# Norm entries of a fused model: three of eight tiles to GpSimd, branch gain at read-out, double-width weighing on VectorE

## What is computed

```python
def rmsnorm(x, g):
    y = x * rsqrt(mean(x * x, axis=-1) + EPS)
    return y * g

h = h + rmsnorm(mix, g[1])
ff = conv_ffn(rmsnorm(h, g[2]), ffn_w_up[l], ffn_conv[l], ffn_w_down[l])
h = h + rmsnorm(ff, g[3])
```

## Time and profile before

| | |
|---|---|
| median of three runs | 1592.94 us (1592.41 to 1594.91) |
| profiled execution, its own time | 1595.38 us |
| span of its profile | 1593.6 us |
| TensorE busy | 1469.6 us, 92% |
| VectorE busy | 1041.1 us, 65% |
| ScalarE busy | 779.9 us, 49% |
| GpSimd busy | 281.6 us, 18% |
| mean granted clock of TensorE | 0.967 |

### The profile page before, as it was taken

How to read it: one execution, slowest core, us unless ns; L and a number is a source line. 1 busy time by engine, 2 the same in 40 slices (tenths; PEclk the granted TensorE clock), 3 DMA queues, 4 the chain that set the end, 5 groups by cost and what they waited for, 6 DMA issues and landing times. The chain is left out here.

```text
span 1593.6 us, 29023 instructions
## 1 busy us (share of the span) xinstructions
PE 1469.6 (92%) x11301; PEld 1404.5 (88%) x11301; DVE 1041.1 (65%) x1727; ACT 779.9 (49%) x1272; POOL 281.6 (18%) x384
## 2 busy tenths in 40 slices
PE   5999879999788898999998899989999989999997
PEld 4999769999686667999997789989999987899997
DVE  5664678877765447788757755357787665677643
ACT  5655644454454444555545555564443555534341
POOL 0000101220053330121100153102332100132110
PEclk8999999999998899999998999999999998999999
DMA  6432535659431224465771311236765733275451
GB/s 275 176 126 106 192 122 193 233 188 335 177 139 74 80 104 162 166 234 211 255 252 58 132 54 54 68 121 222 277 248 208 242 106 137 99 291 185 145 181 44
DMA packets 41141, 265.80 MB, mean 167 GB/s; under 512 B 4561, under 2 KB 5713, under 8 KB 15441
## 3 DMA queue, kind: packets, MB, share of 16 engines
q1 hardware_dynamic: 41040, 264.44, 46.0%
HBM read 263.38 MB, written 1.05 MB: 166 GB/s over the span
## 5 line engine op out<-in xcount | busy, mean ns | idle before, releaser
L224 DVE TENSOR_TENSOR w_lo<-raw,w_hi 128x2048 fp32r<-128x2048 f32 (+2 forms) x207 | 425.4, 2059 | 238.4 <-ACT w_hi L220 234.7
L220 ACT ACTIVATE w_hi<-raw 128x2048 fp32r<-128x2048 f32 (+3 forms) x224 | 385.8, 1727 | 38.1 <-PE bank L398 34.0
L396 PE MATMUL bank<-z_hi,w_hi 128*128 128x258 f32 x752 | 215.4, 286 | 5.1 <-DVEq L931 4.2
L397 PE MATMUL bank<-z_lo,w_hi 128*128 128x258 f32 x752 | 213.0, 283 | 0.0
L398 PE MATMUL bank<-z_hi,w_lo 128*128 128x258 f32 x752 | 212.3, 282 | 0.0
L396 PE MATMUL bank<-x_hi_up,w_hi 128*128 128x272 f32 (+1 forms) x704 | 203.5, 289 | 8.2 <-DVE x_lo_up L688 8.1
L398 PE MATMUL bank<-x_hi_up,w_lo 128*128 128x272 f32 (+1 forms) x704 | 201.7, 287 | 0.0
L397 PE MATMUL bank<-x_lo_up,w_hi 128*128 128x272 f32 (+1 forms) x704 | 201.4, 286 | 0.0
L396 PEld LDWEIGHTS bank<-z_hi,w_hi 128*128 128x128 f32 x752 | 142.1, 189 | 6.7 <-DVE w_lo L224 3.0
L397 PEld LDWEIGHTS bank<-z_lo,w_hi 128*128 128x128 f32 x752 | 143.2, 190 | 0.1
L398 PEld LDWEIGHTS bank<-z_hi,w_lo 128*128 128x128 f32 x752 | 142.4, 189 | 0.0
(11 more groups left out here) (450 smaller groups left out, 3832.1 us busy)
## 6 DMA issues: line engine op xcount, KB each, us to landing
raw<-w_up SPq DMA_DIRECT2D x44, 1024.0 KB, 4.8
raw<-w_gu SPq DMA_DIRECT2D x44, 1024.0 KB, 4.8
work<-w_ada SPq DMA_DIRECT2D x27, 1024.0 KB, 4.9
raw<-w_down SPq DMA_DIRECT2D x32, 704.0 KB, 4.3
raw<-w_dn SPq DMA_DIRECT2D x32, 704.0 KB, 4.1
raw<-w_a_in SPq DMA_DIRECT2D x16, 1024.0 KB, 5.5
mod_w_down<-w_ada SPq DMA_DIRECT2D x12, 1024.0 KB, 6.2
raw<-w_gdn_qkv SPq DMA_DIRECT2D x12, 1024.0 KB, 4.8
```

Of the source, the lines that this page charges most:

```text
L220: act.activation(w_hi[:, s, 0:blocks * P], raw[:, s, 0:blocks * P], ACT.Copy).then_inc(hi_split.sem, 1)
L224: dve.tensor_tensor(w_lo[:, s, 0:blocks * P], raw[:, s, 0:blocks * P], w_hi[:, s, 0:blocks * P].bitcast(F32), ALU.subtract).then_inc(lo_sp ...
L396: pe.matmul(o, w_hi[:, s, b], x_hi[:, xk, cols[0]:cols[1]], start=begin, stop=False)
L397: pe.matmul(o, w_hi[:, s, b], x_lo[:, xk, cols[0]:cols[1]], start=False, stop=False)
```

## The change

- `branch_out` squares all tiles of an item first and then copies them; the copy carries the branch norm's gain as its scale, so what lies in `work` is already weighed with the gain. A semaphore of its own (`branch_taken`) counts the copies.
- In a `NormEntry`, tiles 5, 6 and 7 are GpSimd's. It multiplies them by rstd and adds them to h (residual part), multiplies the gained tile by rstd, and subtracts to x_lo (operand part). The gain of these tiles is applied by ScalarE in three more copies ahead of it. With a shift, ScalarE also writes the shifted tile back.
- VectorE keeps tiles 0 to 4. In the residual part it weighs and adds tiles 0 and 1, 2 and 3 in one instruction each, and tile 4 alone, with tensor_tensor instead of scalar_tensor_tensor.
- ScalarE squares in the order 5, 0, 1, 6, 2, 3, 4, 7 and rounds in the order 0, 5, 1, 6, 2, 3, 7, 4. TensorE's first tile takes k in the order 0, 1, 5, 2, 6, 3, 4, 7.
- In Fox and Gdn GpSimd's entry work comes ahead of its mask and of its small memsets; in Hgrn it comes behind its memsets.
- Waits for all splits now name both engines' semaphores. The unused variants of `NormEntry` are gone.

```diff
+                            for at, k in enumerate(entry.k_order if opening else range(k_tiles)):
                                 b = slice((t * k_tiles + k) * P, (t * k_tiles + k + 1) * P)
                                 xk = k0 + k
-                                begin = xk == 0
-                                end = xk == (FF_TILES if halves else k_tiles) - 1
-                                if entry and isinstance(r, int) and r == first and t == 0:
-                                    pe.wait_ge(entry.split.sem, entry.split.at(k + 1))
+                                begin = k0 + at == 0
+                                end = k0 + at == (FF_TILES if halves else k_tiles) - 1
+                                if opening:
+                                    entry.part_split(pe, k)
                                 if x_ready and isinstance(r, int) and r <= first + 1:
...
-        branch_squared, branch_summed = sig("branch_squared"), sig("branch_summed")
+        branch_squared, branch_summed, branch_taken = sig("branch_squared"), sig("branch_summed"), sig("branch_taken")
+        BRANCH_GAIN = {"a_out": 1, "down0": 3, "b_out": 5, "down1": 7}
 
         def branch_out(name, tiles, cols, squares, halves):
+            gain_at = BRANCH_GAIN[name] * KD
...
                 for t in range(tiles):
+                    slot = s // 2 if halves else j % 2 * 2 + t
+                    act.activation(squares[:, slot, 0:width], where(t)[:, 0:width], ACT.Square).then_inc(branch_squared.sem, 1)
+                for t in range(tiles):
                     at = (j - 1) // 2 if halves else j * tiles + t
                     d = work[:, at, cols[0]:cols[1]] if isinstance(at, int) else work[:, bass.ds(at, 1), cols[0]:cols[1]]
-                    act.activation(d, where(t)[:, 0:width], ACT.Copy)
-                    slot = s // 2 if halves else j % 2 * 2 + t
-                    last = act.activation(squares[:, slot, 0:width], where(t)[:, 0:width], ACT.Square)
-                    last.then_inc(branch_squared.sem, 1)
-                act.wait_ge(branch_squared.sem, branch_squared.at((j + 1) // 2 if halves else (j + 1) * tiles))
+                    act.activation(d, where(t)[:, 0:width], ACT.Copy,
+                                   scale=par("gains", at + gain_at)).then_inc(branch_taken.sem, 1)
+                act.wait_ge(branch_taken.sem, branch_taken.at((j + 1) // 2 if halves else (j + 1) * tiles))
                 act.sem_inc(item_out.sem, 2 if halves else 1)
...
+                normed = residual
+                mine, theirs = n - 3, (n - 3, n - 2, n - 1)
+                square_order = [5, 0, 1, 6, 2, 3, 4, 7] if residual else list(range(n))
+                high_order, self.k_order = [0, 5, 1, 6, 2, 3, 7, 4], [0, 1, 5, 2, 6, 3, 4, 7]
...
+                def part_split(eng, k):
+                    if k < mine:
+                        eng.wait_ge(x_split.sem, x_split.at(k + 1))
+                    else:
+                        eng.wait_ge(p_x_split.sem, p_x_split.at(k - mine + 1))
+
+                def all_split(eng):
+                    eng.wait_ge(x_split.sem, x_split.at(mine))
+                    eng.wait_ge(p_x_split.sem, p_x_split.at(3))
...
+                    for k in square_order:
+                        if normed and k < mine:
+                            act.wait_ge(h_added.sem, h_added.at(k + 1))
+                        elif normed:
+                            act.wait_ge(p_h_added.sem, p_h_added.at(k - mine + 1))
+                        act.activation(work[:, k, c0:c1], src(k), ACT.Square).then_inc(squared.sem, 1)
+                    if act_first:
+                        act_first(act)
+                    act.wait_ge(summed.sem, summed.at(1))
+                    act.activation(std[:, c0:c1], bank[6][:, 0:c1 - c0], ACT.Sqrt, scale=1.0 / count,
+                                   bias=eps_col[:, 0:1]).then_inc(std_made.sem, 1)
+                    for k in theirs:
+                        act.activation(work[:, k, c0:c1], src(k), ACT.Copy, scale=gain(k)).then_inc(x_gained.sem, 1)
+                    for k in high_order:
+                        if k < mine:
+                            act.wait_ge(x_made.sem, x_made.at(k + 1))
+                        else:
+                            act.wait_ge(p_x_made.sem, p_x_made.at(k - mine + 1))
+                        if shift:
+                            ins = act.activation(x_hi[:, k, x_cols], work[:, k, c0:c1], ACT.Identity, bias=shift(k))
+                            if k >= mine:
+                                ins = act.activation(work[:, k, c0:c1], work[:, k, c0:c1], ACT.Identity, bias=shift(k))
+                        else:
+                            ins = act.activation(x_hi[:, k, x_cols], work[:, k, c0:c1], ACT.Copy)
+                        ins.then_inc(x_high.sem, 1)
                     if act_then:
                         act_then(act)
+
+                def low_part(eng, k):
+                    eng.wait_ge(x_high.sem, x_high.at(high_order.index(k) + 1))
+                    hi = x_hi[:, k, x_cols].bitcast(F32)
+                    if shift and k < mine:
+                        ins = eng.scalar_tensor_tensor(x_lo[:, k, x_cols], work[:, k, c0:c1], shift(k), hi, ALU.add,
+                                                       ALU.subtract)
+                    else:
+                        ins = eng.tensor_tensor(x_lo[:, k, x_cols], work[:, k, c0:c1], hi, ALU.subtract)
+                    ins.then_inc((x_split if k < mine else p_x_split).sem, 1)
...
+                    def weigh(k, m):
+                        dve.tensor_tensor(work[:, k:k + m, c0:c1], work[:, k:k + m, c0:c1],
+                                          rstd[:, c0:c1].unsqueeze(1).broadcast_to([P, m, c1 - c0]),
+                                          ALU.mult).then_inc(weighed.sem, m)
+
+                    def add(k, m):
+                        dve.wait_ge(weighed.sem, weighed.at(k + m))
+                        dve.tensor_tensor(h[:, k:k + m, c0:c1], h[:, k:k + m, c0:c1], work[:, k:k + m, c0:c1],
                     if normed:
                         invert()
-                        for k in range(n):
-                            dve.scalar_tensor_tensor(work[:, k, c0:c1], work[:, k, c0:c1], residual[0](k),
-                                                     rstd[:, c0:c1], ALU.mult, ALU.mult).then_inc(weighed.sem, 1)
-                            if k:
-                                add(k - 1)
-                        add(n - 1)
-                    elif residual:
-                        for k in range(n):
-                            dve.scalar_tensor_tensor(h[:, k, c0:c1], work[:, k, c0:c1], residual[0](k),
-                                                     h[:, k, c0:c1], ALU.mult, ALU.add).then_inc(h_added.sem, 1)
+                        weigh(0, 2)
+                        weigh(2, 2)
+                        add(0, 2)
+                        weigh(4, 1)
+                        add(2, 2)
+                        add(4, 1)
                     if dve_first:
                         dve_first(dve)
-                    if stats:
-                        if residual:
-                            dve.wait_ge(h_added.sem, h_added.at(n))
-                        invert()
-                    for k in range(n):
-                        if gain:
-                            dve.scalar_tensor_tensor(work[:, k, c0:c1], src(k), gain(k), rstd[:, c0:c1],
-                                                     ALU.mult, ALU.mult).then_inc(x_made.sem, 1)
-                        if k and x_hi is not None:
-                            low(k - 1)
-                    if x_hi is not None:
-                        low(n - 1)
+                    if normed:
+                        dve.wait_ge(h_added.sem, h_added.at(mine))
+                    invert()
+                    for k in range(mine):
+                        dve.scalar_tensor_tensor(work[:, k, c0:c1], src(k), gain(k), rstd[:, c0:c1],
+                                                 ALU.mult, ALU.mult).then_inc(x_made.sem, 1)
+                        if k:
+                            low_part(dve, k - 1)
+                    low_part(dve, mine - 1)
...
+                def pool(pool):
+                    if normed:
+                        pool.wait_ge(rstd_made.sem, rstd_made.at(1))
+                        for i, k in enumerate(theirs):
+                            pool.tensor_tensor(work[:, k, c0:c1], work[:, k, c0:c1], rstd[:, c0:c1],
+                                               ALU.mult).then_inc(p_weighed.sem, 1)
+                            pool.wait_ge(p_weighed.sem, p_weighed.at(i + 1))
+                            pool.tensor_tensor(h[:, k, c0:c1], h[:, k, c0:c1], work[:, k, c0:c1],
+                                               ALU.add).then_inc(p_h_added.sem, 1)
+                    pool.wait_ge(rstd_made.sem, rstd_made.at(roots))
+                    for i, k in enumerate(theirs):
```

(41 more changed lines are left out.)

91 lines of the change are left out of this document (29 added, 62 removed).

## The result

| | before | changed |
|---|---|---|
| median | 1592.98 us (1592.41 to 1594.91) | 1607.87 us (1605.92 to 1609.85) |
| profiled execution, its span | 1595.38, 1593.6 | 1607.51, 1605.7 |
| mean granted clock of TensorE | 0.967 | 0.958 |

Changed over before: 1.0083, 95% interval 1.0071 to 1.0096. So the change costs 13 us. The prediction had the sign right and the size wrong: 1596.0, with a range that ended at 1601.

What follows compares the result with a forecast made beforehand. TensorE was taken to bound the kernel, except at five layer entries where it waits for VectorE's work and roots. Read-out -1.7, residual +2.4 and operands +2.3 gave +3.0 on 1592.94: 1596.0 us, range 1584 to 1601.

Steps and rivals of the forecast that it cites:

- The exclusion: In the entries, GpSimd and VectorE instructions reading two SBUF tensors take turns: VectorE's hold 0.32 or 0.60 us, GpSimd's 0.575.
- Term A: Residual part, end of first reciprocal to end of last square: 0.58 to 0.88 us later in each of four entries.
- Rival 1: GpSimd and VectorE run side by side in the entries, without excluding each other: -11 us, 1582; 13 in 100.
- rival 2: GpSimd holds only 0.45 us in the entries, or hands over better: 0 down to -3 us, 1591.5; 22 in 100.
- The tail: Last square to second root in a residual entry: a lone last square shortens it by 0.12 us, -0.5 in all.
- The first tile: End of second reciprocal to end of the product's first tile: later operands cost +2.2 us over four residual entries.
- rival 3: TensorE stays at half clock over the first tile in two or three entries: +3 to +5 us, 1600; 20 in 100.
- Fox's body: From Fox's 72nd product matmul to up1's first root: no change counted, 0 us.
- Hgrn: Hgrn's start, which continues behind ScalarE's w_hi splits: +0.1 us.
- Read-out: Read-out of the branch's last tiles up to the first root: squares ahead of copies give -1.7 us in sum.
- Moved past: Fox's mask and Gdn's memsets behind GpSimd's entry work: nothing, or 0.3 us; SP's later wait, +0.4, is covered.
- gained copies: ScalarE's three added copies an entry, 0.5 us each, lie under the reciprocal; uncovered they would cost 1.4 us an entry.

Runs made afterwards that it cites:

- writes_only: The changed kernel with GpSimd's twelve instructions of an entry made memsets, the arithmetic of tiles 5 to 7 left out: 0.9957 of the kernel before, 1588.5 us.
- fill_chg: The changed kernel with matmuls of constants into a spare PSUM bank, 14 ahead of an entry's ones-matmuls and 12 behind: 1.0046 of the kernel before.
- vec_all: The changed kernel with all eight tiles on VectorE, weighed in pairs, and none on GpSimd: 1.0020 of the kernel before.
- readout_only: vec_all with tiles weighed and added one at a time, so the new read-out without double width: 1.0003 of the kernel before.
- fill_chg_more: The changed kernel with more matmuls of constants, 20 ahead of the ones-matmuls and 21 behind: 1.0009 of the kernel before.
- fill_vec2: vec_all with 20 and 17 matmuls of constants an entry: 0.9970 of the kernel before.
- best_fill: vec_all with tiles 4 to 7 weighed singly and matmuls of constants in the entries, ahead of Hgrn's third tile and in Fox: 0.9936, 1584.86 us.

## Why the prediction was wrong

- **The exclusion** (holds of 0.32, 0.60 and 0.575, in turns): right. What the earlier trace rows were set against is in the same trace: the next cast of that tensor, with no VectorE instruction beside it, 0.40 us; the z_lo instruction ahead of the one at 1076.17, 0.48; a w_lo half that GpSimd doesn't meet, 1.19; and the four casts among the eight subtractions:

```profile
1105.74 0.40 POOL L953 CAST a_hi_gu<-prod_gu 128x256 fp32r<-128x256 f32 x1 [0.66 <-DVE prod_gu L945]
...
1075.46 0.48 DVE L579 SCALAR_TENSOR_TENSOR z_lo<-h,mod,z_hi 128x256 fp32r<-128x256 f32 x1 [0.24 <-ACT z_hi L570]
...
861.58 1.19 DVE L2177 TENSOR_TENSOR w_lo<-raw,w_hi 128x1024 fp32r<-128x1024 f32 x1
...
466.08 0.61 POOL L1679 CAST fox_heads<-fox_high 64x272 fp32r<-64x272 f32 x1 [0.16 <-DVE fox_low L1550]
466.75 1.07 POOL L1679 CAST fox_heads<-fox_low 64x272 fp32r<-64x272 f32 x2
467.89 0.51 POOL L1679 CAST fox_heads<-fox_high 64x272 fp32r<-64x272 f32 x1
```

The holds are estimates worked out from such pairs; no trace shows a hold by itself. What the traces show is where the chains of turns end. Up0's splits in the changed kernel, VectorE and the last one of GpSimd:

```profile
216.45 0.99 DVE L694 TENSOR_TENSOR x_lo_up<-work,x_hi_up 128x272 fp32r<-128x272 f32 x1
...
219.05 1.36 DVE L694 TENSOR_TENSOR x_lo_up<-work,x_hi_up 128x272 fp32r<-128x272 f32 x2
...
219.23 0.88 POOL L694 TENSOR_TENSOR x_lo_up<-work,x_hi_up 128x272 fp32r<-128x272 f32 x1 [1.16 <-ACT x_hi_up L682]
```

The last ends at 220.41, 7.21 us after the reciprocal's end at 213.20, where 7.04 was worked out; the last square came 7.64 after the first, where 7.28 was. Term A came out at +3.5 for +2.9; the missing 0.36 in up0 is 0.03 for each of twelve hand-overs, a size that I can only name by that division. The prediction has a slip here: for the narrower up1 and Gdn it took 7.3 "by the same working", but the same turns with holds scaled to 258 and 256 columns end at about 7.0 (an estimate from its own chain). So A should have been about +2.3, and the measured 7.29 and 7.24 met the 7.3 by luck; there too the working was 0.3 short. Rival 1 (side by side) and rival 2 (shorter hold) fell with it. What spoke for rival 1 is one pair of instructions, GpSimd's 0.77 us beside a VectorE instruction that reads PSUM; beside VectorE's readers of two SBUF tensors GpSimd's six in up0's residual part took 0.76 for the first and 0.95 to 1.24 for the others. writes_only gives a limit for rival 1, not its value, since a memset takes 0.32 us where GpSimd's tensor_tensor alone takes 0.72.
- **The tail** (-0.12 an entry): wrong, and the first of the large misses. The 0.73 us of a lone ones-matmul was taken for a latency behind the last square. One alone takes 0.72 us at a clock of 1.00 (fill_chg, at 203.91) and 1.27 at 0.50 (the changed kernel, at 202.84). It is also a rate: back to back four of them take 2.00 us (the a_out row below, clock 1.00), seven take 6.10 at a clock of 0.56 in the changed kernel's up0, and squares that come in bunches queue behind each other. +4.0 instead of -0.5.
- **The first tile** (+2.2): the operands came as late as predicted; the step that failed is the clock. I had it as rival 3 with 8.95 us for the first tile and two or three entries. It was 9.2 in up0 and Fox and 8.8 in up1 and Gdn, all four. The reason given against it, that today's slow stretches end before the tile does, held for the old operand times only: in up0 the clock was 0.69 over the tile before (214.55 to 220.11) and 0.50 after. Before, the slow stretch (0.51 over 215.40 to 218.80) cost nothing, since at 0.225 us a matmul TensorE needs 0.68 for a tile's three and VectorE's scaled tiles come 0.76 apart (216.61, 217.38, 218.14). With the clock held up the tile comes at 8.15, where 7.91 was predicted. What makes the half clock last through the tile is open; the idle time ahead of it is 5.03 us instead of 4.10, but 2.35 in fill_chg gave 0.50 too.
- **Fox's body** (0): not in the sum at all. Nothing in the body is changed, but +3.7 us came there with the lower clock.
- **Hgrn** (+0.1): -1.3, and luck. Its three tiles took 17.9 in the kernel before and 16.6 in the changed one, but 16.4 in vec_all and 17.9 in readout_only, both without a tile on GpSimd. So the change needn't be the reason; the cause is open, and it hid 1.4 us of the miss.
- **Read-out** (-1.7): -0.8. The ends of a_out and down0 in the changed kernel, TensorE and ScalarE:

```profile
195.62 2.00 PE L418 MATMUL bank<-branch_sq_a_out,constants 128*128 128x272 f32 x8
197.92 0.49 ACT L657 ACTIVATE std<-bank,eps_col 128x272 f32<-128x272 f32 x1 [0.66 <-PEq L450]
...
423.22 0.48 ACT L507 ACTIVATE work<-bank,feature_params 128x272 f32<-128x272 f32 x1
424.74 0.49 ACT L657 ACTIVATE std<-bank,eps_col 128x272 f32<-128x272 f32 x1 [1.04 <-PEq L450]
```

In a_out the squares came 0.58 earlier, as predicted, but four tiles' ones-matmuls queue for 2.00 us, and the root starts 0.30 behind the last of them: 0.25 earlier. In down0 the copy is ScalarE's last instruction and the root comes 1.04 behind it, as it came 1.08 behind ScalarE's last before (in a_out and in down0 alike): the copy that was costed at nothing took the square's place, +0.05. b_out gave -0.28, down1 -0.27.
- **Moved past** and the **gained copies**: right, neither shows as a wait.

Together: the step that failed is the clock, which the sum put at nothing in the tail, at the first tile and in Fox's body. They measured +4.0, +6.9 and +3.7 us where -0.5, +2.2 and 0 stood. Where the clock is full at the entries of both kernels, the change costs 3.3 us (0.2 to 6.4), and the sum said 3.0. That this comes out so near is in part luck, since the read-out gave half of what it should and A was mis-sized. The exclusion by itself, fill_chg_more over fill_vec2, is 0.0039, 6 us. The rest of the 13 goes with half clock. Rival 3 named the right cause and was given 0.20 and 1600; it priced one of the three places where the clock bites.

## What to carry to other kernels

Where an entry leaves TensorE idle, look at the granted clock on both sides of the idle time (0.56 over seven sums and 0.50 over the first tile in the changed kernel's up0), and price at half clock too what stands there: the sums, the first tile, and a product behind with gaps of its own, as Fox's body. GpSimd beside VectorE, both reading two SBUF tensors, was no second engine here: 0.39 us of VectorE's time an instruction (16 in 6.2 us) was replaced by a hold on GpSimd estimated at 0.575, and the last square came later, 7.64 us for 6.70. And before a producer is made faster, look at what its consumer needs for all eight tiles, not for the last; here idle-time matmuls of constants and a lone last square took the ratio from 1.0020 to 0.9936.

## What was not expected of the hardware

- Matmuls of constants in idle stretches cost nothing measurable here. In the kernel before, 330 more instructions raised the mean granted clock from 0.967 to 0.979 at 0.9988 of the time; best_fill has 438 more, 0.986 and 0.9936.
- With a granted clock of 0.93 and of 0.90 the same 1102 matmuls of Fox's body are busy for 157.2 and 162.6 us (kernel before, fill_chg_more), and the body takes 176.6 and 182.0.
- GpSimd's memset of 272 columns takes 0.32 to 0.33 us and doesn't slow VectorE beside it: its pair takes 1.36 us with and without.
